# Pair 1 and 2 of the sparse-attention heads: z and gate panels computed feature by feature as one unit of seven half-size products

## The chip, the cores and the metric

One core of one Trainium2 chip. The metric is the device time of one execution, in microseconds. "Kernel before" is the kernel that the change starts from; line numbers (L...) are its lines, except in the diff and where the changed kernel is named.

## What is computed

One mixer layer on x (512 tokens, 1024 features). All three branches read the same normalised input h through one wide projection:

```python
h = rms_norm(x, norm_g[l])
proj = h @ w_in[l]
(qk_a, v_a, if_a, o_a, z_a, q_b, k_b, v_b, z_b, qi, ki, wi, q_m, z_m, gate) = jnp.split(proj, cuts, axis=-1)
...
qb = rotary(rms_norm(q_b.reshape(B, S, DSA_HEADS, DSA_HD), dsa_q_norm_g[l]), positions)
kb = rotary(rms_norm(k_b.reshape(B, S, DSA_HEADS, DSA_HD), dsa_k_norm_g[l]), positions)
y_b = dsa_attention(qb, kb, vb, qib, kib, wib).reshape(B, S, D_DSA) * jax.nn.silu(z_b)
...
g = jax.nn.sigmoid(gate.astype(jnp.float32)).astype(dt).reshape(B, S, N_BRANCH, D_MODEL)
merged = (g[:, :, 0] * (y_a @ w_branch[l, 0]) + g[:, :, 1] * (y_b @ w_branch[l, 1]) + g[:, :, 2] * (y_m @ w_branch[l, 2]))
x = x + merged @ w_out[l]
```

Branch b is the sparse attention: 8 heads of 128 features, 128 chosen keys for each query, and a key mask that was made ahead of this stage.

## The kernel before

Every float32 product is made of three products of rounded parts: high x high, high x low, low x high. An operand's high part is a copy by ScalarE (`b_high`, L1760), its low part the difference original - high by VectorE (`b_low`, L2584). Engines run their own instruction streams and meet at counting semaphores; the order on each engine is written out by hand.

The eight heads of branch b go in four pairs. For pair i there is first a **qkv unit** (`b_unit`, `b_product`, L1185): q, k and v of two heads (2 x 384 columns of `w_in`) as a Strassen-Winograd scheme of seven half-size products instead of eight. Tokens are the outputs' partitions, and a matmul streams 384 columns. Its weight operands are sums and differences of four raw blocks a, b, c, d. GpSimd makes them, four sums of four instructions each (`b_early_sums`, `b_late_sum`, L3169). The sums of tokens (`s_parts`) are made once, ahead. Partial results are saved by ScalarE (`b_save`, `b_last_copy`) and added to others by VectorE (`b_add`, L2591), since there are only four accumulation banks. Three operand slots rotate: the high part of operand n waits until the product that used operand n-3 is done.

Then come two **panels** (`f_panel`, L1214 on; the profile puts its matmuls at L825): 128 columns of z and 256 columns of one gate, by all 512 tokens, all eight k-tiles: 72 matmuls of 512 columns each. Features are the partitions. ScalarE evacuates them with SiLU (`z_evac`, L1819) and Sigmoid (`gate_evac`, L1825), and the gates are stored to HBM.

Between products, **hooks** carry the attention of the heads: for a head a, `b_turn_qk` (L1138, transposes), `b_score` (L1149), `b_turn_p` (L1157), `b_values` (L1167) on TensorE. The even head r of a pair runs in that pair's panels, the odd head (called tail later) in the next pair's qkv unit. What they need is made by VectorE: `b_rotary` (norm sum L2627, four products with the rotary tables L2636, the joining `join` L2398 and L2399, the key scale L2642), `b_values_low` (L2656), `b_qk_low` (L2648, L2650), `b_maxes` (mask and maxima, L2598), `b_scale_p` (L2606, L2609), `b_probs` (L2616), `b_finish` (L2623); by ScalarE: `b_qk_high` (L1807), `b_exps` (L1779), `b_probs_high` (L1799), `b_values_high` (L1788); and by GpSimd: `b_squares` (L3200) and `b_power` (L3205). Operand n of a pair is counted from its unit: 0 to 6 are the seven products, 7 to 10 the panels.

After the four pairs, eight rows of the memory branch come back from HBM (L671) into `merged`, ScalarE splits them (`ym_high`, L1897), and the branch panels begin.

## Time and profile before

| what | before |
|---|---|
| median of 3 runs | 957.01 us (956.84 to 957.34) |
| the profiled execution | 957.17 us |
| its span, first to last instruction | 955.4 us |
| TensorE busy / VectorE / ScalarE / GpSimd | 950.4 / 735.9 / 544.7 / 351.4 us |
| granted TensorE clock | 1.00 of full speed over the span |
| pair 1: qkv unit, panels | 301 to 336 us, 336 to 375 us |
| pair 2: qkv unit, panels | 375 to 409 us, 409 to 448 us |

"Busy" is the time in which an engine has an instruction under way. The timeline gives for each row its start (us from the start of the span), its length, engine, line, what it writes and reads, and in brackets how long the engine had been idle before it and what ended the wait.

### The profile page before, as it was taken

The numbers are of one execution on the slowest core, as the hardware profiler recorded it, in microseconds if no ns is written. First come the engines' busy times: TensorE is split into PE (matmuls) and PEld (weight loads), VectorE is DVE, ScalarE is ACT, GpSimd is POOL, SyncE is SP. The second block draws the span as 40 slices with busy tenths as digits, with TensorE's granted clock in tenths as the row PEclk, the third lists the DMA queues.
The fourth block names the chain that finished last, engine by engine and source line by source line (L and its number), as shares of the span: only waits on it lengthen the run. The fifth ranks groups of instructions, "written<-read, shape, count | busy, mean of one in ns | idle before, by whom it ended". The sixth has DMA issues, their size and how long they took to land.

```text
span 955.4 us, 13764 instructions
## 1 busy us (share of the span) xinstructions
PE 950.4 (99%) x5041; PEld 843.6 (88%) x5041; DVE 735.9 (77%) x1110; ACT 544.7 (57%) x834; POOL 351.4 (37%) x246
## 2 busy tenths in 40 slices
PE   9999999999999999999999999999999999999998
PEld 7888888888989988988988888898998989999887
DVE  6879987688996686685688566796776867984996
ACT  6877644465456546546563422585775957874341
POOL 0200834456227036146120071372613626201930
PEclk9999999999999999999999999999999999999999
DMA  8624222144532531432355324707033150537512
GB/s 286 244 88 132 87 91 70 62 133 133 165 90 66 166 106 60 144 109 78 101 197 177 131 101 155 241 19 214 1 112 120 33 154 1 177 112 299 206 45 88
DMA packets 105158, 119.31 MB, mean 125 GB/s; under 512 B 4772, under 2 KB 80136, under 8 KB 104332
## 3 DMA queue, kind: packets, MB, share of 16 engines
q1 hardware_dynamic: 105084, 118.53, 38.5%
q8 instruction: 36, 0.59, 0.2%
q14 instruction: 22, 0.18, 0.1%
q10 hardware_dynamic: 16, 0.00, 0.0%
HBM read 106.45 MB, written 12.07 MB: 124 GB/s over the span
## 4 chain that ended last, share of the span: by engine, by line
PE 97%; DVE 1%; DMA 1%; POOL 0%; issue 0%; ACT 0%; SPq 0%; POOLq 0%
PE proj L825 41%; PE proj L1185 11%; PE proj L1319 9%; PE att L1340 7%; PE proj L1340 5%; PE att L1430 3%; PE proj L1378 3%; PE proj L995 2%; PE att L1149 2%; PE att L1167 2%; PE att L1092 1%; PE att L1378 1%; PE att L1114 1%; PE proj L1276 1%; PE att L1157 1%; PE att L1138 1%
## 5 line engine op out<-in xcount | busy, mean ns | idle before, releaser
L825 PE MATMUL proj<-hT_hi,w_hi 128*128 128x512 f32 x264 | 104.0, 394 | 0.0
L825 PE MATMUL proj<-hT_hi,w_lo 128*128 128x512 f32 x264 | 103.1, 390 | 0.0
L825 PE MATMUL proj<-hT_lo,w_hi 128*128 128x512 f32 x264 | 102.9, 390 | 0.0
L2233 DVE TENSOR_TENSOR w_lo<-w_raw,w_hi 128x2048 fp32r<-128x2048 f32 x25 | 62.3, 2492 | 42.2 <-ACT w_hi L1480 40.1
L1480 ACT ACTIVATE w_hi<-w_raw 128x2048 fp32r<-128x2048 f32 x24 | 45.9, 1914 | 55.9 <-PE proj L825 54.4
L825 PE MATMUL proj<-y_hi,w_hi 128*128 128x512 f32 x192 | 75.2, 391 | 0.0
L825 PE MATMUL proj<-y_hi,w_lo 128*128 128x512 f32 x192 | 74.8, 390 | 0.0
L825 PE MATMUL proj<-y_lo,w_hi 128*128 128x512 f32 x192 | 74.7, 389 | 0.0
L825 PEld LDWEIGHTS proj<-hT_hi,w_lo 128*128 128x128 f32 x264 | 49.6, 188 | 10.5
L825 PEld LDWEIGHTS proj<-hT_lo,w_hi 128*128 128x128 f32 x264 | 49.6, 188 | 9.9
L825 PEld LDWEIGHTS proj<-hT_hi,w_hi 128*128 128x128 f32 x264 | 49.6, 188 | 9.8
L3169 POOL TENSOR_TENSOR w_raw<-merged,w_raw 128x384 f32<-128x384 f32 x32 | 36.2, 1164 | 54.6 <-DVE w_lo L2584 31.5
L1967 ACT ACTIVATE w_hi<-w_raw 128x1536 fp32r<-128x1536 f32 (+1 forms) x21 | 29.1, 1385 | 40.6 <-DMA w_raw<-w_in_in 13.0
L2801 DVE TENSOR_TENSOR w_lo<-w_raw,w_hi 128x1536 fp32r<-128x1536 f32 (+1 forms) x21 | 35.1, 1669 | 21.9 <-ACT w_hi L1967 21.9
L3241 POOL TENSOR_TENSOR w_raw<-merged,w_raw 128x384 f32<-128x384 f32 x32 | 40.3, 1302 | 29.5 <-DVE w_lo L2801 29.5
L825 PEld LDWEIGHTS proj<-y_hi,w_lo 128*128 128x128 f32 x192 | 36.0, 188 | 7.6
L825 PEld LDWEIGHTS proj<-y_hi,w_hi 128*128 128x128 f32 x192 | 36.1, 188 | 7.4
L825 PEld LDWEIGHTS proj<-y_lo,w_hi 128*128 128x128 f32 x192 | 36.1, 188 | 7.2
L2813 DVE SCALAR_TENSOR_TENSOR negmask<-proj,small,negmask 128x511 f32<-128x511 f32 (+2 forms) x48 | 35.5, 747 | 4.0 <-ACT negmask L2000 2.8
L1319 PE MATMUL proj<-hT_hi,w_hi 128*128 128x512 f32 x96 | 37.6, 392 | 0.0
L1319 PE MATMUL proj<-hT_hi,w_lo 128*128 128x512 f32 x96 | 37.4, 390 | 0.0
L1319 PE MATMUL proj<-hT_lo,w_hi 128*128 128x512 f32 x96 | 37.4, 390 | 0.0
(591 smaller groups left out, 3145.6 us busy)
## 6 DMA issues: line engine op xcount, KB each, us to landing
w_raw<-w_in_in SPq DMA_DIRECT2D x36, 512.0 KB, 4.6
w_raw<-w_in_in SPq DMA_DIRECT2D x56, 256.0 KB, 3.8
w_raw<-w_branch_in SPq DMA_DIRECT2D x12, 1024.0 KB, 6.6
merged<-w_in_in SPq DMA_DIRECT2D x38, 256.0 KB, 3.7
merged<-w_in_in SPq DMA_DIRECT2D x18, 512.0 KB, 6.3
w_raw<-w_mem_kv_in SPq DMA_DIRECT2D x10, 512.0 KB, 7.1
yF<-x_in SPq DMA_DIRECT2D x8, 512.0 KB, 10.5
w_raw<-w_in_in SPq DMA_DIRECT2D x4, 1024.0 KB, 5.0
```

Source lines behind the costliest of these rows:

```text
L825: ins = mm(ps, lhs[a](k, k0), rhs[b](k, k0), start=(first and k == 0 and j == 0), stop=(last and k == KH - 1 and j == 2))
L1185: ins = mm(to[t][:, 0:UNIT_N], lhs[a](k, t), w[b][:, k, :], start=(start and k == 0 and j == 0), stop=(k == KH - 1 and j == 2), skip_group ...
L1319: ins = mm(banks[b][:, :], w[a][:, k, e * P:(e + 1) * P], hT[b_][:, kh * KH + k, :], start=(kh == 0 and k == 0 and j == 0), stop=(kh == 1 ...
L1340: ins = mm(to[t][:, 0:UNIT_N], lhs[a](k, t), w[b][:, k, :], start=(start and k == 0 and j == 0), stop=(k == KH - 1 and j == 2), skip_group ...
L1378: ins = mm(to[f][:, 0:HALF_T], w[a][:, k, f * P:(f + 1) * P], rhs[b](k), start=(start and k == 0 and j == 0), stop=(k == KH - 1 and j == 2 ...
L1480: A_(w_hi[:, kh, :, 0:n], w_raw[:, kh, :, 0:n], ACT.Copy).then_inc(w_hi_done, 1)
L1967: A_(operand(op_hi, n), raw_of(n, first), ACT.Copy).then_inc(op_high, 1)
L2233: V.tensor_tensor(w_lo[:, kh, :, 0:n], w_raw[:, kh, :, 0:n], w_hi[:, kh, :, 0:n].bitcast(F32), ALU.subtract).then_inc(w_lo_done, 1)
L2801: V.tensor_tensor(operand(op_lo, n), raw_of(n, first), operand(op_hi, n).bitcast(F32), ALU.subtract)\
L2813: ins = V.scalar_tensor_tensor(acc[:, lag:], u[:, 0:S - lag], hcw[:, CONV - 1 - lag, b:b + 1], acc[:, lag:], ALU.mult, ALU.add)
L3169: ins = G.tensor_tensor(b_w[out][:, at], b_w[left][:, at], b_w[right][:, at], op)
L3241: ins = G.tensor_tensor(dst[:, at], left[:, at], right[:, at], ALU.subtract)
```

## The change

For the pairs 1 and 2 (`F_UNITS`) the two panels become one **f unit** (`f_unit`): z of both heads and both gates, 2 x 384 columns by 2 x 256 tokens, as seven products of 36 matmuls of 256 columns. Pairs 0 and 3 keep the code they had. With it:

- TensorE: hooks of head r move to other places in the f unit, and in the qkv unit that follows an f unit (`late`) the hooks of the odd head come later.
- GpSimd makes four further sums for each f unit, from four raw blocks of z and gate columns.
- ScalarE saves the parts as they are (`f_save`), VectorE adds (`f_add`), and SiLU and Sigmoid (`f_silu`, `f_sigmoid`) run in the next qkv unit, over SBUF.
- An f unit has seven operands (7 to 13), so `b_high` and `b_low` run 14 instead of 11 times for such a pair. The rotary steps are cut into `b_norm_sum`, `b_turned_parts`, `b_key_scale`, and for heads 2 to 5 the second product of the rotary goes to another buffer, in two halves, so that the joining is four instructions of 256 columns and not two of 512.

```diff
+F_UNITS = (1, 2)
...
+                if i and not late:
                     b_turn_qk(tail)
-                b_product(i, 0, h_block(0, 0), main, True,
-                          lambda t: (bank_empty[t], BF[2][t] + 2 * i) if i else (bank_empty[t], BS[2][t] + 1))
-                if i:
+                b_product(i, 0, h_block(0, 0), main, True, free_main)
+                if i and not late:
                     b_score(tail)
-                b_product(i, 1, h_block(KH, 0), other, True,
-                          lambda t: ((bank_empty[2], BF[2][2] + 2 * i), (u_added, 6 * i))[t] if i else (bank_empty[2 + t], BS[2][2 + t] + 1))
+                b_product(i, 1, h_block(KH, 0), other, True, free_other)
+                if late:
+                    b_turn_qk(tail)
...
                 if i == 0:
                     pe.wait_ge(s_low, 3)
-                b_product(i, 2, h_sum(0), main, False, lambda t: (u_saved, 6 * i + t + 1))
-                if i:
+                b_product(i, 2, h_sum(0), main, False, lambda t: (u_saved, B_S[i] + t + 1))
+                if late:
+                    b_score(tail)
+                elif i:
                     b_turn_p(tail)
-                b_product(i, 3, h_sum(1), main, False, lambda t: (u_saved, 6 * i + t + 3))
-                if i:
+                b_product(i, 3, h_sum(1), main, False, lambda t: (u_saved, B_S[i] + t + 3))
+                if i and not late:
                     b_values(tail)
-                b_product(i, 4, h_sum(2), other, True, lambda t: (u_added, 6 * i + t + 1))
+                b_product(i, 4, h_sum(2), other, True, lambda t: (u_added, B_S[i] + t + 1))
+                if late:
+                    b_turn_p(tail)
                 if i == 0:
                     pe.wait_ge(s_low, 4)
-                b_product(i, 5, h_sum(3), other, False, lambda t: (u_saved, 6 * i + t + 5))
-                b_product(i, 6, h_block(KH, HALF_T), main, False, lambda t: (u_added, 6 * i + t + 3))
+                b_product(i, 5, h_sum(3), other, False, lambda t: (u_saved, B_S[i] + t + 5))
+                if late:
+                    b_values(tail)
+                b_product(i, 6, h_block(KH, HALF_T), main, False, lambda t: (u_added, B_S[i] + t + 3))
...
+            def f_product(i, m, rhs, to, start, before, mid=None):
+                n = B_N[i] + PRODUCTS + m
+                w = [b_op(op, n).rearrange("p (k n) -> p k n", k=KH) for op in (b_op_hi, b_op_lo)]
+                pe.wait_ge(op_low, n + 1)
+                for part, blocks in enumerate(((0,), (1, 2))):
+                    if part and mid is not None:
+                        mid()
+                    pe.wait_ge(*before(part))
+                    for f in blocks:
+                        at = slice((f - blocks[0]) * HALF_T, (f - blocks[0] + 1) * HALF_T)
+                        for k in range(KH):
+                            for j, (a, b) in enumerate(((0, 0), (0, 1), (1, 0))):
+                                ins = mm(to[part][:, at], w[a][:, k, f * P:(f + 1) * P], rhs[b](k),
+                                         start=(start and f == blocks[0] and k == 0 and j == 0),
+                                         stop=(k == KH - 1 and j == 2), skip_group_check=True)
+                    ins.then_inc(u_done, 1)
...
+            def f_unit(i):
+                main, other = (banks[0], banks[1]), (banks[2], banks[3])
+                r, done = 2 * i, B_S[i] + 6
+                f_product(i, 0, f_half_block(0, 0), main, True, lambda t: (u_read, B_R[i] + t + 1))
+                f_product(i, 1, f_half_block(KH, 0), other, True, lambda t: (u_added, B_S[i] + t + 5))
+                f_product(i, 2, f_half_sum(0), main, False, lambda t: (u_saved, done + t + 1), lambda: b_turn_qk(r))
+                b_score(r)
+                f_product(i, 3, f_half_sum(1), main, False, lambda t: (u_saved, done + t + 3))
+                f_product(i, 4, f_half_sum(2), other, True, lambda t: (u_added, done + t + 1))
+                b_turn_p(r)
+                f_product(i, 5, f_half_sum(3), other, False, lambda t: (u_saved, done + t + 5))
+                b_values(r)
+                f_product(i, 6, f_half_block(KH, HALF_T), main, False, lambda t: (u_added, done + t + 3))
...
+            def f_save(i, m, part, src, j, half):
+                th = slice(half * HALF_T, (half + 1) * HALF_T)
+                act.wait_ge(u_done, B_U[i] + 2 * PRODUCTS + 2 * m + part + 1)
+                if part == 0:
+                    act.wait_ge(yb_sent[j], SENT0 + 16 * i)
+                    return A_(f_z(i, j)[:, th], src[0][:, 0:HALF_T], ACT.Copy)
+                for b in range(2):
+                    act.wait_ge(gate_sent[b], SENT0 + 16 * (2 + 2 * i))
+                return A_(f_gates(j)[:, :, th], src[1][:, :].rearrange("p (b n) -> p b n", b=2), ACT.Copy)
...
+                if i - 1 in F_UNITS:
+                    f_silu(i - 1)
+                    b_high(n + 2)
+                    act.wait_ge(b_vlow, 2 * i)
+                    b_save(i, 0, main, b_raw[:, 0:2])
+                    b_high(n + 3)
                     b_qk_high(tail)
-                b_high(n + 2)
-                if i:
-                    act.wait_ge(b_vlow, 2 * i)
-                b_save(i, 0, (banks[0], banks[1]), b_raw[:, 0:2])
-                b_high(n + 3)
-                if i:
+                    f_sigmoid(i - 1)
+                    b_save(i, 2, main, b_second)
+                    b_high(n + 4)
+                    b_high(n + 5)
                     b_exps(tail)
-                b_high(n + 4)
-                if i == 0:
-                    act.wait_ge(kept, 32)
-                b_save(i, 2, (banks[0], banks[1]), b_second)
-                b_high(n + 5)
-                if i:
+                    b_high(n + 6)
+                    b_save(i, 4, other, b_fifth)
                     b_probs_high(tail)
...
+                    f_save(i, 0, 0, main, 0, 0).then_inc(u_saved, 1)
+                    f_save(i, 0, 1, main, 0, 0).then_inc(u_saved, 1)
+                    b_high(n + 9)
+                    b_high(n + 10)
+                    f_save(i, 2, 0, main, 1, 0).then_inc(u_saved, 1)
+                    b_qk_high(r)
+                    f_save(i, 2, 1, main, 1, 0).then_inc(u_saved, 1)
+                    b_high(n + 11)
+                    b_exps(r)
+                    b_high(n + 12)
+                    f_save(i, 4, 0, other, 1, 1).then_inc(u_saved, 1)
+                    b_high(n + 13)
+                    f_save(i, 4, 1, other, 1, 1).then_inc(u_saved, 1)
+                    b_probs_high(r)
+                    b_high(n + 14)
+                    b_high(n + 15)
+                    b_values_high(l)
+                    f_save(i, 6, 0, main, 0, 1).then_inc(u_read, 1)
+                    f_save(i, 6, 1, main, 0, 1).then_inc(u_read, 1)
...
+                if i - 1 in F_UNITS:
+                    b_turned_parts(tail)
+                    b_values_low(tail)
+                    b_low(n + 2)
+                    b_key_scale(tail)
+                    b_finish(tail - 1)
+                    b_low(n + 3)
                     b_qk_low(tail)
-                b_low(n + 2)
-                rounds(1, 4)
-                if i:
+                    b_add(i, 1, (banks[2], banks[3]), b_raw[:, 0:2], 1)
+                    b_low(n + 4)
                     b_maxes(tail)
-                b_low(n + 3)
-                b_add(i, 1, (banks[2], banks[3]), b_raw[:, 0:2], 1)
-                if i:
+                    b_low(n + 5)
+                    b_low(n + 6)
                     b_scale_p(tail)
-                rounds(2, 1)
-                b_low(n + 4)
-                if i:
                     b_probs(tail)
-                rounds(2, 2)
-                b_low(n + 5)
-                b_low(n + 6)
-                if i:
+                    b_add(i, 3, (banks[0], banks[1]), b_fifth, 5)
+                    b_low(n + 7)
+                    b_add(i, 5, (banks[2], banks[3]), b_second, 3)
+                    b_low(n + 8)
                     b_finish(tail)
...
+                    b_norm_sum(r)
+                    b_turned_parts(r)
+                    b_low(n + 9)
+                    b_key_scale(r)
+                    b_low(n + 10)
+                    b_values_low(r)
+                    b_qk_low(r)
+                    f_add(i, 1, other, 0, 0, 1)
+                    b_maxes(r)
+                    b_low(n + 11)
+                    b_norm_sum(l)
+                    b_scale_p(r)
+                    b_low(n + 12)
+                    b_low(n + 13)
+                    f_add(i, 3, main, 1, 1, 5)
+                    b_probs(r)
+                    b_low(n + 14)
+                    f_add(i, 5, other, 1, 0, 3)
+                    b_low(n + 15)
...
+                if i in F_UNITS:
+                    b_first_sums(i, 1)
+                    b_squares(2 * i)
+                    b_second_sum(i, 1)
+                    b_power(2 * i)
+                    b_third_sum(i, 1)
+                    b_late_sum(i, 1)
+                    b_squares(2 * i + 1)
+                    b_power(2 * i + 1)
+                    b_early_sums(i + 1)
...
```

Where the instructions stand now, at the three places that matter below.

GpSimd, pair 1, from the last sum of the qkv unit on. `arena<-yF` are the squares of a head, `small<-small,minus_half` its norm's power, the others weight sums. Before:

```order
L3169 TENSOR_TENSOR w_raw<-merged,w_raw 128x384 [waits op_low,t_done]
L3169 TENSOR_TENSOR w_raw<-merged,w_raw 128x384 x3
L3200 TENSOR_TENSOR arena<-yF 128x512 [waits b_out,u_added]
L3200 TENSOR_TENSOR arena<-merged 128x512
L3205 TENSOR_TENSOR small<-small,minus_half 128x8 [waits b_norm_steps]
L3200 TENSOR_TENSOR arena<-arena 128x512 [waits b_vlow,u_read,u_added]
L3200 TENSOR_TENSOR arena<-arena 128x512
L3205 TENSOR_TENSOR small<-small,minus_half 128x8 [waits b_norm_steps]
```

Now:

```order
L3408 TENSOR_TENSOR w_raw<-merged,w_raw 128x384 [waits raw_d_landed,raw_b_landed]
L3408 TENSOR_TENSOR w_raw<-merged,w_raw 128x384 x3
L3452 TENSOR_TENSOR arena<-yF 128x512 [waits b_out,u_added]
L3452 TENSOR_TENSOR arena<-merged 128x512
L3408 TENSOR_TENSOR w_raw<-w_raw 128x384 [waits op_low,t_done]
L3408 TENSOR_TENSOR w_raw<-w_raw 128x384 x3
L3457 TENSOR_TENSOR small<-small,minus_half 128x8 [waits b_norm_steps]
L3408 TENSOR_TENSOR merged<-merged,w_raw 128x384 [waits op_low,t_done]
L3408 TENSOR_TENSOR merged<-merged,w_raw 128x384 x3
L3408 TENSOR_TENSOR w_raw<-merged,w_raw 128x384 [waits op_low,t_done]
L3408 TENSOR_TENSOR w_raw<-merged,w_raw 128x384 x3
L3452 TENSOR_TENSOR arena<-arena 128x512 [waits b_vlow,u_read,u_added]
```

Four sums of four instructions stand between and around the squares and the power.

VectorE, the changed kernel, from the last operand of pair 1's f unit into pair 2's qkv unit (lines of the changed kernel: L2746 low parts, L2811 the rotary products, L2560 and L2561 the joining, L2852 the low values, L2824 the key scale):

```order
L2746 TENSOR_TENSOR w_lo<-merged,w_hi 128x1536 [waits op_high]
L2811 TENSOR_TENSOR arena<-arena,tabs 128x512 [waits b_turned]
L2811 TENSOR_TENSOR arena<-arena,tabs 128x512
L2811 TENSOR_TENSOR w_lo_f_71<-arena,tabs 128x512 x2
L2560 TENSOR_TENSOR arena<-arena,w_lo_f_71 128x4x64 [waits dve_step]
L2561 TENSOR_TENSOR arena<-arena,w_lo_f_71 128x4x64
L2560 TENSOR_TENSOR arena<-arena,w_lo_f_71 128x4x64
L2561 TENSOR_TENSOR arena<-arena,w_lo_f_71 128x4x64
L2852 TENSOR_TENSOR b_vl<-arena,b_vh 128x256 [waits b_vhigh,dve_step]
L2852 TENSOR_TENSOR b_vl<-arena,b_vh 128x256
L2746 TENSOR_TENSOR w_lo<-w_raw,w_hi 128x1536 [waits op_high]
L2824 TENSOR_TENSOR arena<-arena,small 128x4x128 [waits b_norm_steps]
```

Before, the rotary of the odd head stood inside the panels, ahead of head r's maxima, and at this place was only this:

```order
L2623 TENSOR_TENSOR w_raw<-att,w_raw 128x512 [waits bank_empty0,b_out]
L2656 TENSOR_TENSOR b_vl<-arena,b_vh 128x256 [waits b_vhigh]
L2656 TENSOR_TENSOR b_vl<-arena,b_vh 128x256
L2648 TENSOR_TENSOR b_ql<-att,b_qh 128x512 [waits b_qhigh]
L2650 TENSOR_TENSOR b_kl<-att,b_kh 128x512 [waits b_khigh]
```

VectorE, the odd head's step from maxima to scaled probabilities (`small<-small` with `b_masked` is the bias for the exponentials, RECIPROCAL begins the scaling). Before:

```order
L2602 TENSOR_TENSOR small<-small 128x4 [waits b_masked]
L2584 TENSOR_TENSOR w_lo<-w_raw,w_hi 128x1536 [waits op_high]
L2591 TENSOR_TENSOR arena<-proj,arena 128x384 [waits u_done,u_saved] x2
L2606 RECIPROCAL small<-small 128x4 [waits b_exp]
L2609 TENSOR_SCALAR score<-score,small 128x128 [waits dve_step]
```

Now, in a qkv unit that follows an f unit (L2764, L2768 and L2771 are those lines in the changed kernel):

```order
L2764 TENSOR_TENSOR small<-small 128x4 [waits b_masked]
L2746 TENSOR_TENSOR w_lo<-merged,w_hi 128x1536 [waits op_high]
L2746 TENSOR_TENSOR b_op_lo_75<-merged,b_op_hi_74 128x1536 [waits op_high]
L2768 RECIPROCAL small<-small 128x4 [waits b_exp]
L2771 TENSOR_SCALAR score<-score,small 128x128 [waits dve_step]
```

Two low parts stand between bias and scaling, and the high part of the second comes on ScalarE behind the exponentials.

## Rows read from the trace of the kernel before

**Rows 1.** The page: busy time of the engines, and the chain that ended last, by engine.

```profile
PE 950.4 (99%) x5041; PEld 843.6 (88%) x5041; DVE 735.9 (77%) x1110; ACT 544.7 (57%) x834; POOL 351.4 (37%) x246
...
PE 97%; DVE 1%; DMA 1%; POOL 0%; issue 0%; ACT 0%; SPq 0%; POOLq 0%
```

**Rows 2.** Waits on TensorE: who waited for whom, us in total, times, longest.

```profile
PE att L978 <- POOL ident L3107: 1.5, 1, 1.5
```

**Rows 3.** The chain in order of time: start us, us, what.

```profile
409.47 8.21 PE proj L825 x36
417.67 0.87 PE att L1138 x8
...
424.02 1.91 PE att L1149 x12
...
436.84 1.09 PE att L1157 x10
...
443.43 1.85 PE att L1167 x12
...
455.02 8.33 PE proj L1185 x48
...
834.97 11.51 PE proj L1378 x96
```

**Rows 4.** Timeline of VectorE and GpSimd: steps with the other engine's sums absent.

```profile
362.99 3.94 POOL L3169 TENSOR_TENSOR w_raw<-merged,w_raw 128x384 f32<-128x384 f32 x4 [12.95 <-DVE b_op_lo L2584]
...
403.08 1.76 DVE L2584 TENSOR_TENSOR w_lo<-w_raw,w_hi 128x1536 fp32r<-128x1536 f32 x1 [0.82 <-ACT w_hi L1760]
...
410.97 0.69 DVE L2636 TENSOR_TENSOR arena<-yF,tabs 128x512 f32<-128x512 f32 x1
411.58 0.69 DVE L2636 TENSOR_TENSOR arena<-merged,tabs 128x512 f32<-128x512 f32 x1
...
415.72 0.43 DVE L2656 TENSOR_TENSOR b_vl<-yF,b_vh 128x256 fp32r<-128x256 f32 x1
416.06 0.42 DVE L2656 TENSOR_TENSOR b_vl<-merged,b_vh 128x256 fp32r<-128x256 f32 x1
```

**Rows 5.** Timeline of VectorE and GpSimd: both at work at once.

```profile
372.55 2.33 DVE L2656 TENSOR_TENSOR b_vl<-arena,b_vh 128x256 fp32r<-128x256 f32 x2
...
379.84 0.29 DVE L2598 CUSTOM_DVE_ANT_0 score<-att,negmask 128x128 f32<-128x128 f32 x1 [0.57 <-PE att L1149]
...
382.35 2.60 POOL L3169 TENSOR_TENSOR w_raw<-merged,w_raw 128x384 f32<-128x384 f32 x1
...
634.60 1.50 DVE L2945 TENSOR_TENSOR a_ql<-tabs,a_qh 128x512 fp32r<-128x512 f32 x1
...
635.51 1.46 POOL L3241 TENSOR_TENSOR merged<-merged,w_raw 128x384 f32<-128x384 f32 x1
```

**Rows 6.** Timeline: the steps from maxima to scaled probabilities, and one high part.

```profile
395.14 1.49 ACT L1760 ACTIVATE b_op_hi<-merged 128x1536 fp32r<-128x1536 f32 x1 [2.17 <-PE proj L1185]
...
426.16 0.29 DVE L2598 CUSTOM_DVE_ANT_0 score<-att,negmask 128x128 f32<-128x128 f32 x1
...
427.93 0.16 DVE L2602 TENSOR_TENSOR small<-small 128x4 f32<-128x4 f32 x1
...
433.54 1.27 DVE L2609 TENSOR_SCALAR score<-score,small 128x128 f32<-128x128 f32 x4
...
501.52 0.49 ACT L1779 ACTIVATE score<-score,small 128x128 f32<-128x128 f32 x1 [0.22 <-DVE small L2602]
...
504.00 0.18 ACT L1779 ACTIVATION_READ_ACCUMULATOR score<-score,small 128x1 f32 x1
```

**Rows 7.** SyncE's copy of the memory rows, its landing, and ScalarE's first use of them.

```profile
473.08 0.37 SPq L671 DMA_DIRECT2D merged<-ym_kept  x1
...
DMA to landing us min/median/max: 7.1/7.1/7.1
...
483.48 2.18 ACT L1897 ACTIVATE y_hi<-merged 128x512 fp32r<-128x512 f32 x4
```

286 lines of the change are left out of this document (212 added, 74 removed).

## The prediction, made before the changed kernel ran

> **What bounds the kernel now.** I read the page first: TensorE is busy for 950.4 of 955.4 us and holds 97% of the chain that ended last [rows 1]. Then the waits on TensorE: the longest is 1.5 us, at the start, and none in the pairs [rows 2]. So what the change takes from TensorE's work shows one for one in the time, and so does every wait that it brings. Whether it brings any is read from the other engines' timelines, by order and length. The granted clock is 1.00 throughout. The reader should keep both questions apart: how much matmul time goes, and who delivers late afterwards.
>
> **What TensorE saves.** Two panels are 144 matmuls of 512 columns; 36 of them take 8.21 us, so 0.228 us each and 32.8 us for a pair [rows 3]. An f unit is 7 x 36 = 252 matmuls of 256 columns; 96 of that form take 11.51 us, so 0.120 each and 30.2 us [rows 3]. The hooks stay as they are in number. That is 2.6 us for a pair, **5.1 us** for both. Evacuations and table loads are ScalarE's, which is busy 57% [rows 1]; I cost them only where somebody waits.
>
> **The price of VectorE and GpSimd at once.** Alone, a VectorE product of 512 columns over SBUF follows another after 0.61 us, one of 256 columns after 0.34, a low part takes 1.76 (1.67 behind another step), and a GpSimd instruction of a weight sum about 1.0 (3.94 for four) [rows 4]. Together they take turns: 512 columns then take 1.50 and GpSimd's instruction 1.46, two of 256 columns 2.33, and a GpSimd instruction that asks while a low part is under way, 2.60 [rows 5]. So whoever asks waits for the other's instruction: a round is about 1.43 us, of which 0.61 is VectorE's and 0.82 GpSimd's. A mask step, one of whose inputs is in PSUM, takes 0.29 beside a sum and 0.29 without [rows 5, 6]; such steps I count free of turns. The rows show only up to a few rounds in a row, so the length of longer stretches is an estimate from them. The Trainium skill has a rule that speaks against the change (SBUF — State Buffer, "Who interferes with whom"): a VectorE instruction with two SBUF inputs and a GpSimd one that reads SBUF exclude each other for the whole instruction. By it every step in a long stretch pays a full round, the sum below; the weaker reading of the rows is rival 4. The change puts 32 more GpSimd instructions, 16 for each f unit, right beside the rotary steps, where before GpSimd made only squares and powers.
>
> **First f unit, step by step.** Times are us after its first product begins (409.47 in rows 3 and 4 for the same place of the next pair; everything up to here is as before). TensorE alone would be at operand 2 at 8.64 (two products of 36 x 0.120), at the end of that product with its transposes at 13.8, and done at 36.0.
> - VectorE can begin the rotary at 1.5 [rows 4]. GpSimd's squares end at 0.1 and its second sum begins at once. Four rotary products in turn with four GpSimd instructions end at 6.1, four joining steps at 8.4 (the third sum comes in from 7.2), one more GpSimd instruction, then the low part of operand 2: 9.25 to 10.9. TensorE asked at 8.64: **wait 2.3**. Without turns it would be 8.2: no wait.
> - Behind it on VectorE: key scale 12.4 (the transposes need it just then), low part of operand 3 14.9, low values 17.2, and q and k low 18.45, each behind one GpSimd instruction where both inputs lie in SBUF. TensorE, 2.3 late, wants the scores at 16.15: **wait 2.3**. After that ScalarE and VectorE are ahead to the end of the unit, at 40.6.
>
> **The qkv unit behind it** (it begins at 40.6 and wants the odd head's transposes after two products, 24 x 0.1735 us each [rows 3], at 48.9). GpSimd's sums for it can begin once the low part of its operand 0 is made, 34.4. VectorE is free for the odd head's rotary at about 38. Then come 4 products, 4 joining steps, 2 low values, each in turn with one of 12 GpSimd instructions: 50.8. Low part of operand 2 to 52.5, one instruction of the last sum, key scale to 53.95. **Wait 5.0.** Alone VectorE would be through at 46, so here too turns decide.
>
> Then the scaling. From the end of the scores, s: ScalarE saves and makes the high parts of operands 4 and 5, VectorE the low part of 4 (to s+1.9), maxima and bias 1.9 [rows 6], the exponentials 2.66, high part of operand 6 1.4, its low part 1.7, reciprocal and first scaling 0.4: the first scaled block is there at s+10.1, the last transposes end at about s+11.6. TensorE, after two products (8.3) and 1.09 of transposes, wanted to be at s+9.4. **Wait 2.2**, with or without turns.
>
> **Second f unit.** The odd head's values now stand before the last product, so the partial sums, squares and norm are ready about 2.5 us earlier: no wait for operand 2. The chain to q and k low is 7.5 us behind that low part as before (8.4 to 15.9), against 13.8: **wait 2.1**. The qkv unit of pair 3: again 5.0 and 2.2.
>
> **Queues.** SyncE's copy of the memory rows stands behind the store of head 5, whose finish is now behind the last low part: issued about 8 us later than at 473.08. It took 7.1 us, and ScalarE wants it 10.4 us after the issue [rows 7]: about 5 us late there, and the first branch operand with it. TensorE is still 11.8 us away from it: I take 0.5 us (0 to 3). The f units' raw blocks are asked for four to seven low parts ahead: no wait.
>
> **Sum.** Waits 4.6 + 5.0 + 2.2 + 2.1 + 5.0 + 2.2 + 0.5 = 21.6; less 5.1 of matmuls: +16.5 us. Against the profiled execution, 957.17 (its span 955.4 and 1.8 around it), 973.7; the median shown is 957.01, 0.2 less. **Forecast 973.5 us.** The unknown with the widest bounds is how strictly the two engines take turns through long stretches: no turns at all gives waits of 4.4 to 5, nothing gained or lost (957); every step behind a full round gives the sum above, and one more sum instruction ahead at each of the six waits (0.8) some 5 us more (979). I take the strict turns, since the rows where both stay busy are nearest to these stretches.
>
> **Rivals.**
> 1. *The clock falls in the new waits.* Before, TensorE never pauses for more than 1.5 us [rows 2], so no row shows what its clock does after 5 us without work. If it drops from 2.4 to 1.2 GHz and the product behind each of the two long waits (4.2 us) runs at the lower level, that is up to 8.4 us: 982. For it: the waits are long. Against: no row. The Trainium skill (TensorE: Matmul & The Clock Gate, "What's actually happening") says that the gate halves the clock after idleness; by it the time would be this one. Chance 0.14.
> 2. *The turns hardly matter* (GpSimd's sums run before or after VectorE's steps): only the scaling wait is left, 2 x 2.2 and 0.5 against 5.1: 957, within 0.2% of before. For it: for the steps alone VectorE is in time in both places. Chance 0.08.
> 3. *Faster: TensorE also gets its scaled blocks in time.* The chain behind the scores would have to be 2.2 us shorter, by maxima that run before the low part of operand 4 is due, and the turns would have to hide; then the matmuls' 5.1 us come through: 952. It decides from all waits together below 5.1 us. Against: the hand-written order puts the maxima behind that low part, and the high part of operand 6 behind the exponentials. Chance 0.07.
> 4. *Half of it:* the squares and sums start somewhat earlier than I lay them, and each of the four turn-bound waits is half: 966. Chance 0.15.
>
> **Chances and range.** Strict turns 0.56, with 968 to 980. What a measurement of this kernel can tell from no change is about 0.2%, 1.9 us. Faster 0.07, the same 0.08, slower 0.85. The range leaves out rivals 2 and 3 and the far end of rival 1: 962 to 982.
>
> **What would show it.** Right: the waits on TensorE list four of some 2 to 5 us on VectorE (low part of operand 2, q and k low, key scale) and two on the scaling at L2771; VectorE's rotary products last about 1.4 us while GpSimd's sums run; the f units' matmuls take 30.2 us net of waits. The clock row shows rival 1. Wrong: TensorE busy to the end of both f units without such waits, or a wait on a DMA or on GpSimd's sums in their place.

## The result, and the profile after

The changed kernel took **987.48 us** (median; 986.76 to 989.28), the kernel before 956.92 beside it: a ratio of 1.0322 (95% interval 1.0304 to 1.034), 30.6 us slower. The forecast was 973.5, with 962 to 982 as its range: the sign is right, the size is not. The profiled span is 987.1 us.

The page's busy row, against [rows 1], and the waits on TensorE, against [rows 2] (us in total, times, longest):

```profile
PE 958.7 (97%) x5257; PEld 861.2 (87%) x5257; DVE 778.8 (79%) x1136; ACT 552.7 (56%) x850; POOL 393.5 (40%) x278
```

```profile
PE att L1181 <- DVE arena L2824: 7.7, 2, 3.9
PE att L1192 <- DVE b_kl L2846: 6.2, 2, 3.1
PE att L1200 <- DVE score L2771: 5.2, 5, 1.6
PE proj L1295 <- DVE w_lo L2746: 2.8, 1, 2.8
PE att L1021 <- POOL ident L3346: 1.5, 1, 1.5
PE proj L1295 <- DVE b_op_lo L2746: 1.4, 1, 1.4
PE proj L868 <- issue: 0.8, 1, 0.8
```

L1181 are the transposes of q and k, L1192 the scores, L1200 the transposes of the probabilities, L1295 the products of the f units, L2824 the key scale, L2846 k low, L2771 the scaling. All but the fifth are new: 24.1 us, where 21.6 were predicted. Eight of the nine places were named; operand 2 of the second f unit (1.4) was not, and the last row (0.8) stands where the memory rows were expected. (The kernel before had three short waits of its own, 0.7 us together.) Waits of 24.1 are not enough for 31.7 us of span. TensorE is also busy for 8.3 us more than before, though its matmuls should be 5.1 us shorter. The trace cut into stretches, around six of the eight places where TensorE waits for VectorE, shows why (the column behind the engines is the granted clock as a share of 2.4 GHz):

```profile
355.00:360.00 5.00, 4.72 (x22) 4.52 (x23) 3.31 (x13) 1.36 (x2) 1.78 (x2) 0.66 0.15 39
390.00:400.00 10.00, 8.51 (x44) 8.42 (x45) 6.98 (x10) 8.02 (x12) 5.76 (x4) 0.83 0.40 138
410.00:415.00 5.00, 2.91 (x13) 2.25 (x14) 4.34 (x7) 1.59 (x4) 4.20 (x4) 0.83 0.51 157
440.00:450.00 10.00, 6.87 (x33) 6.41 (x32) 8.15 (x17) 2.79 (x5) 5.97 (x5) 0.70 0.31 81
480.00:485.00 5.00, 3.16 (x13) 3.16 (x14) 4.96 (x6) 3.52 (x6) 3.67 (x3) 0.66 0.13 50
500.00:505.00 5.00, 4.57 (x20) 4.23 (x21) 4.70 (x12) 2.70 (x5) 0.00 (x0) 0.70 0.00 0
```

Behind the waits TensorE runs at 1.2 GHz for a while (1-us slices read 0.50), where it never did before. In the first row 0.34 of 5 us is missing, 1.7 us of work. It is about the same in the other places (the third and the last run on past their stretch), but for the fourth, where 0.30 of 10 us is 3.0 and the next five still read 0.92. The mean clock of the span is 0.988, so it costs 0.012 x 987.1 = **11.8 us**. The sum: 955.4 - 5.1 + 24.1 + 11.8 = 986.2, against 987.1.

The first f unit's timeline (start, length) shows the turns. Before, such products took 0.69 [rows 4]:

```profile
337.77 0.68 DVE L2811 TENSOR_TENSOR arena<-yF,tabs 128x512 f32<-128x512 f32 x1
338.37 1.50 DVE L2811 TENSOR_TENSOR arena<-merged,tabs 128x512 f32<-128x512 f32 x1
339.80 1.50 DVE L2811 TENSOR_TENSOR w_lo_f<-yF,tabs 128x512 f32<-128x512 f32 x1
341.22 0.68 DVE L2811 TENSOR_TENSOR w_lo_f<-merged,tabs 128x512 f32<-128x512 f32 x1
...
344.24 2.43 DVE L2746 TENSOR_TENSOR w_lo<-w_raw,w_hi 128x1536 fp32r<-128x1536 f32 x1
346.59 1.50 DVE L2824 TENSOR_TENSOR arena<-arena,small 128x512 f32<-128x512 f32 x1
348.01 0.96 DVE L2825 TENSOR_SCALAR small<-small 128x4 f32<-128x4 f32 x1
...
353.86 0.68 DVE L2844 TENSOR_TENSOR b_ql<-att,b_qh 128x512 fp32r<-128x512 f32 x1
```

```profile
335.83 4.92 POOL L3408 TENSOR_TENSOR w_raw<-w_raw 128x384 f32<-128x384 f32 x4
...
342.77 6.17 POOL L3408 TENSOR_TENSOR merged<-merged,w_raw 128x384 f32<-128x384 f32 x4
349.02 5.76 POOL L3408 TENSOR_TENSOR w_raw<-merged,w_raw 128x384 f32<-128x384 f32 x4
```

Beside a sum a step takes about 0.8 us more (0.68 to 1.50), and four of GpSimd's instructions 4.9 to 6.2 us and not 3.94 [rows 4]. Q low, which reads PSUM, keeps its 0.68. From 335.9 us to the end of k low, at 355.1, VectorE stands idle nowhere: it is late because its steps are long, and not because it waits for a sum.

### The profile page after: what moved, and what is told of

It reads as the page before. It is cut to its first block, busy times and chain, and to the rows that moved or that the text cites. A ratio compares the mean times of both kernels' runs of the same rounds, so it can differ in the third digit from the quotient of the medians.

```text
span 987.1 us, 14306 instructions
## 1 busy us (share of the span) xinstructions
PE 958.7 (97%) x5257; PEld 861.2 (87%) x5257; DVE 778.8 (79%) x1136; ACT 552.7 (56%) x850; POOL 393.5 (40%) x278
## 4 chain that ended last, share of the span: by engine, by line
PE 84%; DVE 8%; issue 3%; ACT 2%; DMA 2%; POOL 1%; SPq 0%; DVEq 0%; ACTq 0%; POOLq 0%
PE proj L868 33%; PE proj L1421 9%; PE proj L1228 7%; PE att L1442 7%; PE proj L1442 5%; PE att L1532 3%; PE proj L1480 3%; PE proj L1038 2%; PE att L1192 2%; DVE w_lo L2746 1%; PE proj L1295 1%; DMA merged<-w_in_in 1%; PE att L1135 1%; PE att L1480 1%; PE att L1157 1%
## 5 line engine op out<-in xcount | busy, mean ns | idle before, releaser
L3408 POOL TENSOR_TENSOR w_raw<-merged,w_raw 128x384 f32<-128x384 f32 x48 | 59.1, 1262 | 75.7 <-DMA merged<-w_in_in 38.7
L868 PE MATMUL proj<-hT_hi,w_hi 128*128 128x512 f32 x192 | 75.6, 394 | 0.0
L868 PE MATMUL proj<-hT_hi,w_lo 128*128 128x512 f32 x192 | 75.0, 390 | 0.0
L868 PE MATMUL proj<-hT_lo,w_hi 128*128 128x512 f32 x192 | 74.8, 390 | 0.0
L3504 POOL TENSOR_TENSOR w_raw<-merged,w_raw 128x384 f32<-128x384 f32 x32 | 40.2, 1294 | 29.5 <-DVE w_lo L3040 29.5
L2129 ACT ACTIVATE w_hi<-w_raw 128x1536 fp32r<-128x1536 f32 (+1 forms) x21 | 29.1, 1385 | 40.5 <-DMA w_raw<-w_in_in 11.8
L3040 DVE TENSOR_TENSOR w_lo<-w_raw,w_hi 128x1536 fp32r<-128x1536 f32 (+1 forms) x21 | 35.0, 1669 | 20.8 <-ACT w_hi L2129 20.8
L868 PEld LDWEIGHTS proj<-hT_hi,w_lo 128*128 128x128 f32 x192 | 36.0, 188 | 7.7
L868 PEld LDWEIGHTS proj<-hT_lo,w_hi 128*128 128x128 f32 x192 | 36.1, 188 | 7.2
L868 PEld LDWEIGHTS proj<-hT_hi,w_hi 128*128 128x128 f32 x192 | 36.1, 188 | 7.2
L2746 DVE TENSOR_TENSOR w_lo<-w_raw,w_hi 128x1536 fp32r<-128x1536 f32 (+1 forms) x19 | 37.4, 1970 | 5.7 <-ACT w_hi L1863 5.4
L1421 PE MATMUL proj<-hT_hi,w_hi 128*128 128x512 f32 x96 | 37.6, 392 | 0.0
L1421 PE MATMUL proj<-hT_lo,w_hi 128*128 128x512 f32 x96 | 37.4, 390 | 0.0
```

What stands on the lines that cost most here:

```text
L868: ins = mm(ps, lhs[a](k, k0), rhs[b](k, k0), start=(first and k == 0 and j == 0), stop=(last and k == KH - 1 and j == 2))
L1421: ins = mm(banks[b][:, :], w[a][:, k, e * P:(e + 1) * P], hT[b_][:, kh * KH + k, :], start=(kh == 0 and k == 0 and j == 0), stop=(kh == 1 ...
L2746: V.tensor_tensor(b_op(b_op_lo, n), b_raw_of(n), b_op(b_op_hi, n).bitcast(F32), ALU.subtract).then_inc(op_low, 1)
L3040: V.tensor_tensor(operand(op_lo, n), raw_of(n, first), operand(op_hi, n).bitcast(F32), ALU.subtract)\
L3408: ins = G.tensor_tensor(b_w[out][:, at], b_w[left][:, at], b_w[right][:, at], op)
L3504: ins = G.tensor_tensor(dst[:, at], left[:, at], right[:, at], ALU.subtract)
```

## The experiments

**Theory of the whole difference:** turns between VectorE and GpSimd and a hand-written order make eight waits, and each wait can drop the clock. **Rivals:** VectorE's own order alone; a clock that falls on its own account; a cost that no wait shows.

**1. TensorE kept at work through the waits (e_warm).**

```diff
+            def fill(n, *held):
+                pe.wait_ge(*held)
+                for _ in range(n):
+                    mm(att[3][:, :], hT[0][:, 0, 0:P], hT[0][:, 0, :], start=True, stop=True)
...
+                fill((8, 4)[i - 1], b_pcopied, 4 * r)
                 f_product(i, 2, f_half_sum(0), main, False, lambda t: (u_saved, done + t + 1), lambda: b_turn_qk(r))
```

> The changed kernel with TensorE kept at work through the eight new waits: 8 (unit 1) or 4 (unit 2) spare products of 128x512 by hT into an unused bank before operand 2 of each f unit, 9 before its scores, 14 before the late transposes of q and k, 6 before the late transposes of the probabilities (60 in all; nothing reads them). They start once the step before is done, so where they fit they fill the wait and add no time of their own. Theory (the clock falls because TensorE stands idle, and costs about 12 us over six stretches): about 975 us, clock 1.00 throughout, the waits themselves unchanged in place. Rival (the fall is not tied to idle stretches, or the spare products only lengthen the path): 987 us or more.

Measured: 980.78 us, span 979.2, 7.9 less than the changed kernel's, though work was added (the spare products are 70, not 60: 12 + 18 + 28 + 12). Stretches of its trace:

```profile
355.00:360.00 5.00, 3.92 (x29) 3.75 (x29) 4.74 (x14) 2.23 (x4) 2.66 (x3) 1.00 0.33 92
390.00:400.00 10.00, 9.26 (x58) 9.02 (x58) 7.98 (x11) 9.15 (x13) 5.77 (x4) 1.00 0.48 157
410.00:415.00 5.00, 4.41 (x19) 4.02 (x20) 4.10 (x9) 2.60 (x4) 2.29 (x3) 0.66 0.33 112
```

The clock stays up in five of six places. The mean is 0.998, a cost of 2.0 us and not 11.8, so 9.8 came back. The 70 spare products (17.4 us busy) and what is left of the waits (8.6) make 26.0 against 24.1: 1.9 given away. 9.8 - 1.9 is the 7.9. The falls belong to idle TensorE. The one that stayed came where the spare products were used up and TensorE then stopped four times, for the scaled blocks, for 0.56, 0.67, 0.63 and 0.24 us: no single long wait is needed. The expected 975 overlooked this fall and the lengthened path.

**2. The late scaling ahead of the low parts (e_scale).**

```diff
+                    b_maxes(tail)
                     b_low(n + 4)
-                    b_maxes(tail)
+                    b_scale_p(tail)
                     b_low(n + 5)
                     b_low(n + 6)
-                    b_scale_p(tail)
```

(and ScalarE's `b_exps(tail)` ahead of `b_high(n + 5)`)

> The changed kernel with the late scaling moved ahead of the raw and low parts: in the late tail ScalarE makes the exponentials right behind the high part of the first operand, and VectorE the maxima before the first low part and the scaling before the second. Theory (the late transposes of the probabilities wait because the scaling stands behind the low parts): that wait of 3.5 and 1.6 us and the two falls of the clock behind it (about 3.4 us) go: about 979 us. Rival (the wait moves to the low parts, which are now later, or to the key scale): no less than 985 us.

Measured: 980.73 us, against 979 expected. No wait on the scaling is left, so its cause is the place in the order. Operand 2 of the second f unit now waits 4.9 us and not 1.4, since TensorE comes earlier and VectorE does not.

**3. The sums cut to 8 columns (e_nosum), and with the scaling moved as well (e_nosum_scale).**

```diff
+            def b_weight_sum_cut(out, left, right, op):
+                at = slice(0, 8)
+                G.tensor_tensor(b_w[out][:, at], b_w[left][:, at], b_w[right][:, at], op).then_inc(t_done, 1)
...
-                b_weight_sum("a", "b", "a", ALU.add)
+                (b_weight_sum_cut if second or i - 1 in F_UNITS else b_weight_sum)("a", "b", "a", ALU.add)
```

The same is done for the first, third and late sums: for each f unit its four sums and the first three of the unit behind it, 14 sums in all. The result of these kernels is not the layer's.

> The changed kernel with GpSimd's weight sums beside the f units and before the unit behind each cut from 512 to 8 columns (those sums are left out of the computation). Everything else keeps its order. Theory (VectorE takes turns with GpSimd, and so operand 2, q and k low and the late key scale are late): those waits, some 14 us, and the falls of the clock behind them, some 8 us, go, and the late scaling alone is left: 962 to 966 us. Rival (the order of VectorE's own steps is what makes them late): no less than 980 us.

> The weight sums of the run before this one cut to 8 columns (left out of the computation) and, with it, the late scaling moved ahead of the low parts. Theory (all eight waits are turn-taking or the place of the scaling, and nothing else keeps the change from giving its 5.1 us): 951 to 953 us, faster than the kernel before, no fall of the clock. Rival (there is a cost that no wait shows): 956 us or more.

Measured: 961.00 (1 us under the lower bound) and **952.55 us** (ratio 0.9956, interval 0.9936 to 0.9975). In the first the scaling is the only new wait on VectorE; in the second there is none:

```profile
PE att L1200 <- DVE score L2771: 3.9, 2, 2.0
```

```profile
PE 945.5 (99%) x5257; PEld 851.1 (90%) x5257; DVE 745.6 (78%) x1136; ACT 550.6 (58%) x850; POOL 324.4 (34%) x236
```

TensorE is busy 945.5 us, 4.9 less than before: the matmuls give what was predicted. VectorE is busy 33.2 us less than in the changed kernel with the same number of instructions: that is what the turns with these 14 sums take from it, about 2.4 us for each. The rival of the order alone falls (it wanted 980 or more), and so does a large cost that no wait shows (it wanted 956 or more; experiment 7 finds a small one). Cutting a sum takes away the turns and also the time until its result is there. For the waits on the low parts and on the key scale it is the turns, as pair 1 in the changed kernel shows: VectorE worked without a pause from 335.9 to 355.1 us, and again from 377.3 us until the late key scale, at 391.4: 14.1 us for steps that by the prediction's prices take 6.8 alone.

**4. One f unit only (e_one).**

```diff
-F_UNITS = (1, 2)
+F_UNITS = (1,)
```

> Only pair 1 as an f unit, pair 2 as before. Theory (each f unit and the unit behind it bring the same kinds of waits and falls of the clock, less 2.6 us of matmuls): about half of the difference and somewhat more, since the waits of the first f unit are the longer ones: 972 to 975 us. Rival (the cost comes from two such units in a row, the second taking over what the first left late): below 966 us.

Measured: 969.19 us, 12.3 over before: 40% of the difference, under the expected half and above the rival's 966. Its waits are 2.9, 0.4, 3.9 and 1.6. The second, on k low, is 3.1 in the changed kernel at the same place. The stretch from 345 to 355 us shows why; the changed kernel, then this one:

```profile
345.00:350.00 5.00, 3.28 (x28) 3.28 (x29) 4.97 (x5) 1.42 (x3) 4.92 (x5) 1.00 0.00 0
350.00:355.00 5.00, 2.16 (x19) 1.96 (x17) 5.00 (x5) 0.82 (x3) 5.00 (x5) 1.00 0.44 123
```

```profile
345.00:350.00 5.00, 3.02 (x14) 3.02 (x15) 4.96 (x5) 0.06 (x1) 4.92 (x4) 0.62 0.00 0
350.00:355.00 5.00, 5.00 (x32) 4.94 (x30) 5.00 (x5) 1.52 (x3) 5.00 (x4) 0.70 0.41 108
```

The code up to there is the same, and so is the wait ahead of it (2.8 and 2.9). In one profile the clock fell behind it, in the other not, and where it fell the slower product used up the next wait. So a fall is not bound to a length of wait, and its cost hides where a wait follows.

**5. Other orders of the complete kernel (f_a, f_b, f_abs).**

```diff
+                    dve.wait_ge(u_added, B_S[i] + 6)
+                    b_turned_parts(r)
                     b_norm_sum(r)
-                    b_turned_parts(r)
...
                     b_first_sums(i, 1)
+                    b_second_sum(i, 1)
                     b_squares(2 * i)
-                    b_second_sum(i, 1)
```

> The changed kernel, complete, with the f units in another order: GpSimd makes the second sum before the squares instead of behind them, VectorE makes the rotary products and joins before the sum of squares, and q and k low before the low values. So the second sum runs beside no rotary step. Theory (order and turns together make operand 2 and q and k low late): those four waits, 10.4 us in all, and three of the six falls of the clock, some 5 us, go: 970 to 974 us. Rival (the third sum takes the place of the second, and the rotary is as late as before): 982 us or more.

```diff
-                    b_turned_parts(tail)
                     b_values_low(tail)
                     b_low(n + 2)
-                    b_key_scale(tail)
...
+                    b_turned_parts(l)
+                    b_key_scale(l)
                     b_probs(r)
                     b_low(n + 14)
```

> The changed kernel, complete, with the odd head's rotary and key scale inside the f unit, before the low parts of the probabilities, instead of behind operand 1 of the next unit, beside GpSimd's early sums. Theory (that wait is due to the turns with the early sums): the two waits on the key scale, 7.7 us, and their two falls of the clock, 3.4 us, go: 975 to 978 us. Rival (the steps are only late elsewhere: the low parts of the f unit become the wait): 985 us or more.

> The changed kernel, complete, with all three new orders at once: the f units' sums and rotary, the odd head's rotary inside the f unit, and the late scaling ahead of the low parts. Theory (the change itself is sound, and only the order of VectorE's and GpSimd's steps loses the time): no wait over 1 us but the one at the start, clock 1.00, 952 to 956 us. Rival (VectorE has no room for these steps beside GpSimd in any order): 965 us or more.

Measured: 981.34, 987.23 and 976.18 us. In all three I had looked for too much: f_b and f_abs came in as their rivals said, and f_a within 1 us of its rival. In f_a the rotary products still took 1.5 us each, beside the second sum's end and the squares. In f_b the wait on the key scale is gone and TensorE waits as long elsewhere, on the low probabilities behind the moved steps and on the scaling (4.8, before 5.2):

```profile
PE att L1192 <- DVE b_kl L2846: 6.2, 2, 3.1
PE att L1210 <- DVE b_pl L2778: 5.5, 2, 2.8
PE att L1200 <- DVE score L2771: 4.8, 2, 2.4
```

**6. Who makes the sum (f_c, f_c2, f_d, f_e).**

```diff
-                    b_second_sum(i, 1)
...
+            def b_second_sum_here(i):
+                dve.wait_ge(t_done, B_T[i] + 5)
+                dve.wait_ge(op_low, B_N[i] + PRODUCTS + 1)
+                V.tensor_tensor(b_w["a"][:, 0:1536], b_w["b"][:, 0:1536], b_w["a"][:, 0:1536], ALU.add).then_inc(t_done, 1)
```

> The changed kernel, complete. The f units' second sum is one VectorE instruction of 1536 columns before the low part of operand 1, instead of four of GpSimd's; GpSimd's third sum waits for the key scale; q and k low stand before the low values; the odd head's rotary and key scale stand in the f unit behind the low parts of the probabilities; the late scaling is ahead of the low parts. Theory (a sum costs VectorE 1.7 us when it makes it itself, and up to 3.3 us of turns when GpSimd does, so this takes the remaining waits of the run before): 952 to 957 us, no wait over 1 us but the first, clock 1.00. Rival (the third and late sums, now later, make operand 4 late): waits of over 2 us on the low part of operand 4, 960 us or more.

> The same, but GpSimd's third sum does not wait for the key scale and so runs beside the rotary joins and the low part of operand 2. Theory (each of its four instructions holds VectorE up by one turn of 0.8 us there): operand 2 or the key scale late by 1 to 3 us in both f units, so 3 to 8 us above the run before it. Rival (VectorE has slack there): the same time within 1 us.

> The kernel of f_c with four more moves: GpSimd's third sum starts behind the low part of operand 2 instead of behind the key scale; the sum of squares stands between the rotary products and the joins; the first two sums of the unit behind an f unit are VectorE's, one instruction each, in the idle time that it has there; GpSimd keeps the third and the late one. Theory (what is left of the waits in f_c is the lateness of two sums, on the low part of operand 4 and on that of operand 2 of the unit behind): those waits, 10 us together, and the falls of the clock behind them go, 953 to 958 us. Rival (VectorE is now the bound and the waits come elsewhere): 963 us or more.

> The kernel of f_d with the f units' third sum also one VectorE instruction, behind the key scale, q and k low ahead of the low part of operand 3, and in the second f unit the first sum VectorE's too, where it stood idle for 2.9 us waiting for GpSimd's. GpSimd keeps the late sum alone in the f units (and the first in pair 1). Theory (the two waits left on the low part of operand 4 and the one on operand 2 of the second f unit, 4.8 us, are GpSimd's late sums, and VectorE has the room): no wait over 1 us but the first and one of 1.1 that waits for nothing shown, clock 1.00: 952 to 956 us, faster than the kernel before. Rival (VectorE is full): waits of over 1.5 us on its low parts elsewhere and 960 us or more.

Measured: 971.65, 974.40, 963.29 and **959.96 us** (f_e: ratio 1.003, interval 1.0018 to 1.0041). VectorE's own second sum takes 1.74 us in f_c, where GpSimd's four instructions took 4.92 in the changed kernel with VectorE's steps slowed beside them, and the rotary products behind it keep to 0.69:

```profile
331.44 1.74 DVE L2859 TENSOR_TENSOR w_raw<-w_raw 128x1536 f32<-128x1536 f32 x1
...
338.57 0.69 DVE L2811 TENSOR_TENSOR arena<-merged,tabs 128x512 f32<-128x512 f32 x1
339.18 0.68 DVE L2811 TENSOR_TENSOR w_lo_f<-yF,tabs 128x512 f32<-128x512 f32 x1
```

f_c2, without the gate on the third sum, waits 3.8 and 5.3 us for operand 2 of the two f units, and is 2.8 us slower than f_c, just under its lower bound of 3. From f_c to f_d to f_e each step helped, and each fell short of its number. Operand 4 waits 2.4 and 2.2 us in f_c, 2.0 and 2.8 in f_d, and 1.3 twice in f_e, where VectorE makes the third sum: a late sum was part of it, not all. In f_e the granted clock is 1.00, and 6.1 us of waits are left: 2.6 for operand 4 and 0.4 and 1.9 for operand 2 of the two f units, and 1.2 in the last panel.

**7. The copy of the memory rows, and the last orders (f_h, f_i, f_i1, f_j, f_j1).**

```diff
             sp.dma_start(merged[:, 0:6 * S], ym_kept[:, 0:6 * S]).then_inc(kept_back, 16)
+            y_store(2 * PAIRS - 3)
             sp.wait_ge(op_low, n + 9)
```

> The kernel of f_e with four more moves in the order: the even head's low values go behind the low part of operand 4 (they took 2.5 us in turns with GpSimd's late sum ahead of it), the low part of operand 2 stands before the rotary joins, the late finish of the second f unit behind the key scale, and SyncE asks for the memory rows of the last pair before it stores the late head, not behind it. Theory (each wait left in f_e is one of these orders: 3.2 us on operand 4, 1.9 on operand 2 of the second f unit, 1.2 before the last panel's second operand, which the trace names issue and which I put down to the late copy): TensorE waits 1 us or less in all of them, 952 to 955 us, faster than the kernel before by over 0.2%. Rival (the waits move to the key scale, now behind the joins, and the 1.2 us are not the copy's): 956 us or more.

Measured: 961.30 us, 1.3 more than f_e and not the 952 to 955 expected. The copy is settled. In f_e ScalarE waited 5.4 us for it, and TensorE 1.2 before the last panel's second operand; in f_h neither waits. ScalarE in f_e, then in f_h:

```profile
490.50 2.20 ACT L2059 ACTIVATE y_hi<-merged 128x512 fp32r<-128x512 f32 x4 [5.43 <-DMA merged<-ym_kept]
```

```profile
488.50 2.18 ACT L2060 ACTIVATE y_hi<-merged 128x512 fp32r<-128x512 f32 x4
```

The rest of f_h moved small waits about (its text puts 3.2 us on operand 4; it was 2.6), and left more of them: ten stops on VectorE in these units where f_e has six.

Then the late sum, shown here against f_h:

```diff
-                    b_late_sum(i, 1)
...
+                    b_late_sum_here(i)
                     f_add(i, 1, other, 0, 0, 1)
+                    b_low(n + 11)
                     b_maxes(r)
-                    b_low(n + 11)
                     b_values_low(r)
```

> The kernel of f_h with the f units' late sum a VectorE instruction as well, behind the low part of operand 3; the low part of operand 4 ahead of the maxima, the low values behind them, the late finish ahead of the rotary joins, the sum of squares of the odd head ahead of the low part of operand 5. GpSimd now makes none of the second, third and late sums of the f units. Theory (what is left of the waits comes from turns with the late sum, some 2 us per f unit, for which a VectorE sum is 1.7): the waits of f_h on q and k low, operand 4 and the low probabilities (4 us) go, 955 to 957 us. Rival (VectorE has no room left in the f units, whoever makes the sums): 959 us or more.

> The same with pair 1 alone as an f unit, pair 2 as before the change. Theory (in the first f unit VectorE comes in with slack, in the second it comes in late, since the unit between them also carries two more sums and the late head): 2.6 us of matmuls against about 1.5 of waits, 955 to 956.5 us, about 0.1% below the kernel before. Rival (each f unit costs more than its matmuls give back, in either place): 957.5 us or more.

Measured: 963.73 and 959.81 us, both in their rivals' range, each f unit with one wait of 2.3 us on operand 5, made by that order. The last pair of runs takes it away (shown against f_i):

```diff
                     b_high(n + 11)
+                    b_high(n + 12)
                     b_exps(r)
-                    b_high(n + 12)
```

> The kernel of f_i with one place changed in the f units: ScalarE makes the high part of operand 5 ahead of the exponentials, where it was idle for 3.7 us, and VectorE its low part in the 2.1 us in which it waited for them. Theory (the two waits of 2.3 us in f_i are that order alone, and the clock falls behind them): both waits and the fall go, some 6 us: 956 to 958 us, no wait over 1 us but the first, clock 1.00. Rival (VectorE has no room, the wait goes to operand 6 or to the low probabilities): 960 us or more.

> The same with pair 1 alone as an f unit. Theory: 2.6 us of matmuls against 0.5 of waits and what the breaks between them cost: 955 to 956 us, faster than the kernel before by about 0.1%. Rival (an f unit costs more than its matmuls also without waits): 957 us or more.

Measured: 961.60 and **958.96 us** (f_j1: ratio 1.0019, interval 1.001 to 1.0028), clock 1.00 in both. The two waits and the falls behind them went as the theory said, and yet both times are the rivals'. The waits of f_j:

```profile
PE att L1201 <- DVE score L2772: 2.4, 4, 0.7
PE att L1022 <- POOL ident L3383: 1.5, 1, 1.5
PE proj L1229 <- DVE w_lo L2747: 1.4, 3, 0.6
PE att L1182 <- DVE arena L2827: 1.1, 2, 1.0
PE att L1211 <- DVE b_pl L2779: 1.1, 2, 0.6
PE att L929 <- DMA merged<-mem_in: 0.3, 1, 0.3
PE proj L1229 <- DVE b_op_lo L2747: 0.2, 1, 0.2
```

Twelve new short stops, 6.2 us, none over 1.0: more than the 5.1 us of matmuls. And TensorE is busy 948.7 us, 3.2 more than in e_nosum_scale at the same clock: some 0.27 us for each stop on top of its wait. The rows around a stop show where that lies. In the changed kernel, at operand 2 of the first f unit:

```profile
343.54 0.28 PE L1295 MATMUL proj<-hT_lo,b_op_hi 128*128 128x256 f32 x1
343.66 0.28 PE L1295 MATMUL proj<-hT_hi,b_op_lo 128*128 128x256 f32 x1
346.72 0.39 PE L1295 MATMUL proj<-y_hi,w_hi 128*128 128x256 f32 x1 [2.79 <-DVE w_lo L2746]
346.95 0.28 PE L1295 MATMUL proj<-y_lo,w_hi 128*128 128x256 f32 x1
```

In a stream these matmuls start every 0.12 us though each is shown for 0.28: they overlap. Before a stop nothing overlaps the last one, which is 0.16 more; behind it the second starts 0.23 and not 0.12 after the first, 0.11 more. Together 0.27. The starts alone say the same: 3.29 us from the second row to the fourth, where a stream takes 0.24, so 3.05 lost for a wait shown as 2.79. No complete version of mine beats the kernel before, and whether an order exists that does stays open; the run with cut sums puts what it could give at some 4.2 us (956.73 - 952.55).

## Why the prediction was right and wrong

- **Matmuls, 5.1 us:** right. TensorE's busy time is 4.9 less where nothing disturbs it (experiment 3).
- **The price of the turns:** right in kind: 1.50 for the products, as in [rows 5]. The Trainium skill (SBUF — State Buffer, "Who interferes with whom") says that a VectorE instruction with two SBUF inputs contends with a GpSimd one that reads SBUF, and one with at most one SBUF input outside the two-port modes does not; the rows agree, 1.50 for the products and 0.68 for q low. But not every step pays the full round: of the first f unit's four rotary products two took 0.68.
- **Operand 2 of the first f unit:** 2.3 predicted, 2.8 measured. **Q and k low:** 2.3 and 2.1 predicted, 3.1 and 3.1 measured. **Operand 2 of the second f unit:** none predicted, 1.4 measured.
- **Key scale of the odd head:** 5.0 predicted, 3.9 and 3.8 measured. A wait that I had excluded is inside it: the raw block of operand 15 landed late, ScalarE stood 2.8 us for it, VectorE 1.45 for ScalarE, and the rotary began only at 377.3. "The f units' raw blocks are asked for [...]: no wait" was wrong; I had counted low parts, not the time from the landing.

```profile
373.74 1.49 ACT L1863 ACTIVATE w_hi<-merged 128x1536 fp32r<-128x1536 f32 x1 [2.80 <-DMA merged<-w_in_in]
```

- **Late scaling:** 2.2 predicted for each, 3.5 (1.64, 0.67, 0.63 and 0.59) and 1.6 measured; "with or without turns" held (3.9 for both with the sums cut). **Memory rows:** 0.5 predicted, 0.8 measured, cause confirmed by f_h.
- **The sum of waits** is thus 24.1 for 21.6, 2.5 us off.
- **The step that failed is the clock.** The prediction left it out of the sum and made it rival 1, with a chance of 0.14, two places and at most 8.4 us. It was 11.8 us in six places, behind waits of 1.6 and 3 us too. The ground for the low chance was "no row". But a kernel that never pauses has no such row to show, so its absence spoke neither for nor against. The Trainium skill (TensorE: Matmul & The Clock Gate, "What's actually happening") has the gate halve the clock after idleness, and the trace agrees in the direction; with its term in the sum the forecast would have been 982 by the rival's own working, the edge of the range and still 5.5 too low. Together: 973.7 + 2.5 + 11.8 + 0.9 unexplained = 988.9, against 989.28 for the profiled execution (the last 0.4 lies outside its span). The prediction has no term for the stops themselves either. At 0.27 us each (experiment 7) the eleven stops on VectorE would come to 3.0 and more than fill the 0.9, so the account closes to some 2 us, not better.

## What to carry to other kernels

A kernel whose TensorE never pauses pays more than once for a wait: its length, and the clock behind it (here 11.8 us on 24.1). Each stop adds some 0.27 us more. Price all of it, and take the absence of a row about the clock for ignorance, not for safety. Before work is given to GpSimd because it is idle, count how much VectorE work with two SBUF inputs stands beside it: here a sum was 1.7 us on VectorE, and cost it about 2.4 in turns when GpSimd made it. When a change saves a few us of the bound engine spread over many handovers, ask whether the engine that feeds it has room at each of them, not on average: VectorE was 79% busy and late in eight places.

## What the runs showed of the hardware that was not expected

- Very small VectorE steps can pay the turns too: the `TENSOR_SCALAR` over 128x4 at L2825, with one tile as input, takes 0.96 us beside a sum, 0.16 without (f_c). The sum of squares (`TENSOR_REDUCE`) does not: 1.22 beside the second sum, as before the change.
- GpSimd's power over 128x8 takes 1.64 us alone and 3.08 beside a low part (f_i).

```profile
362.89 3.08 POOL L3494 TENSOR_TENSOR small<-small,minus_half 128x8 f32<-128x8 f32 x1 [2.75 <-DVE small L2796]
```

- The same wait at the same place (2.7 to 2.9 us before operand 2 of the first f unit) dropped the clock in e_one and e_scale and not in the changed kernel and f_b. The code up to there is the same in all four. So whether a wait brings a fall is a chance here, and the next wait can hide the cost.
